# Five ring slots for the gathered rows, and the residual kept in its own memory

## The chip, the cores and the metric

One core of a Trainium2 chip runs the whole program, written in Bass with its waits and queues by hand. The metric is the device time of one execution in microseconds, median of the runs; the profile is one more execution.

## The reference, cut to what matters

One layer of a decoder over 512 prompt tokens and 64 sample tokens (8 sequences of 8), width 1024: a hybrid mixer, attention over memory tokens, then PEER, a layer of 16384 single-neuron experts. The change is in PEER:

```
q = (x @ wq).reshape(N, 8, 2, 64)                  # 8 heads, two half queries
s = einsum('thpd,hpkd->thpk', q, keys)             # 128 keys for each half
sv, si = top_k(s, 16); cv, ci = top_k(all 256 sums, 16)
eidx = i1 * 128 + i2                               # 8 x 16 = 128 experts a token
gate = softmax(cv)
h = gelu(sum_d u_tab[eidx] * x)                    # one dot product each
out = sum_k (gate * h) * v_tab[eidx];  y = rmsnorm(residual + out)
```

u_tab and v_tab have 16384 rows of 1024 floats, in float32.

## The kernel before, in words

hT holds the residual, transposed: 128 partitions x 8 blocks x 576 tokens. The mixer and the attention add to it. PEER then works on two groups of tokens in two ways.

**Dense.** The first 384 prompt tokens go through all experts. peer_experts runs 128 steps j: step j takes one 512 KB tile of the u table, in a high part (ACT, L1835) and a low part (POOL, L1803), multiplies it by the tokens in three products (PE, L1921), and ACT applies gelu (L1864) and stores the activations to DRAM (acts). peer_output runs 128 steps e over v (1 MB loads of two), weighted by activations times gates. DVE chooses the experts of these tokens (select) and spreads their gates into dense matrices from step FIRST_SPREAD = 85 on, three groups of four tokens to a step (L2078, L2080).

**Gathered.** The other 128 prompt tokens and the 64 sample tokens are done pick by pick: 128 picks for the prompt tokens, 64 for the samples (two halves of the picks on 128 partitions), 192 in all. For pick n (counted from 0) POOL fetches by an indirect DMA the 8 KB row (u and v side by side) of the expert of each of 128 partitions into a ring slot, 1 MB in all (fetch, L1514). DVE forms the dot product with u (product, L1521), ACT the gelu and the gate (weigh, L1527 and L1529), and DVE adds v times the weight to a sum (add, L1540); add of pick n-2 follows the product of pick n. A slot is free for fetch n when add of pick n - SLOTS is done; POOL waits for that.

SLOTS is 7. Five slots are memory of their own (40 KB a partition, which also serves peer_scores as nT and qT), and two lie in hT. Because these overwrite the residual, peer_scores stores hT whole to a DRAM tensor (saved, L1585), and SP waits for it. peer_output loads the columns it needs back into hC, in eight DMAs at the steps 1, 3, 5 and 7 (L2154, L2155), after a wait for the last stored activations, and PE adds them by products with the identity (L2236 after step 16, L2244 at the end).

**Order.** Every engine works its list in the order written. ACT's step j: wait until PE has finished the product of step j-1, gelu of it, the high part of tile j+2, a store, parts of the gates' spreading, then the weighings of the picks of step j. POOL's step j: the low part of tile j+2, then the fetches of step j. In the spread steps POOL first waits for DVE's one-hot matrices. pick_step(n) gives ACT's step for pick n: 20 + 4n/3 up to pick 45, step 84 for 46 and 47, one to a step for 48 to 79 (steps 85 to 116), two to a step for 80 to 99 (steps 117 to 126). POOL's step for fetch n is 13 for the first SLOTS of them, and else

```
before = n - gather.SLOTS
step = 13 if before < 0 else pick_step(min(before + 2, LOOP_PICKS - 1)) + 1
```

so with seven slots one step after the weighing of pick n-5. The picks 100 to 191 are worked in peer_output, three for every four steps, and there POOL has only fetches in its list. The picks and their order in time can be counted in the trace: the n-th instruction of L1514, L1521 or L1529 is that of pick n-1.

In peer_output DVE also makes the low part of every v row (L2264), the weighting (L2255) and its low part (L2259), ACT the high parts (L2192, L2198).

Of the kernel before, what the change touches and what calls it, by code (L numbers as in the profile page):

```python
# [24 lines left out]
P = 128  # L25
D = 1024
# [1454 lines left out]

class Gather:

    FIXED = 5
    SLOTS = 7

    def __init__(self, nc, ctx, sem, hT):
        sb = lambda n, s, dt=F32: ctx.enter_context(nc.sbuf_tensor("ga_" + n, s, dt))
        self.ring = sb("ring", [P, self.FIXED, 2 * D])
        h_flat = hT[:, :, :].rearrange("p k n -> p (k n)")  # L1490
        self.slots = [self.ring[:, i] for i in range(self.FIXED)] + \
                     [h_flat[:, i * 2 * D:(i + 1) * 2 * D] for i in range(self.SLOTS - self.FIXED)]
        self.flat = self.ring[:, :, :].rearrange("p a b -> p (a b)")
        self.x = sb("x", [P, 2, D])
        self.idx = sb("idx", [P, NPICK], U32)
        self.gate = sb("gate", [P, NPICK])
        self.dot = sb("dot", [P, NPICK])
        self.act = sb("act", [P, NPICK])
        self.weight = sb("weight", [P, NPICK])
        self.landed = [sem(f"ga_landed{i}") for i in range(self.SLOTS)]  # L1500
        self.dots, self.gelus, self.weights, self.summed = (sem("ga_dots"), sem("ga_gelus"), sem("ga_weights"),
                                                            sem("ga_summed"))
# [46 lines left out]
def peer_scores(nc, io, sem, hT, cst, gains, ps, xhi, xlo, scores, gather):  # L1549

    CHUNKS = 2 * DT + 3
    with ExitStack() as ctx:
        def sb(name, shape, dt=F32):
# [13 lines left out]
        score_mm, score_out, high, dve_seq = (sem("ps_score_mm"), sem("ps_score_out"), sem("ps_high"),  # L1567
                                              sem("ps_dve_seq"))
        doubled, q_zero, q_doubled = sem("ps_doubled"), sem("ps_q_zero"), sem("ps_q_doubled")
        turned, turned_out, acc_ready, saved = (sem("ps_turned"), sem("ps_turned_out"), sem("ps_acc_ready"),  # L1570
                                                sem("ps_saved"))
        ident = cst[:, C_ID:C_ID + P]
        block = ctx.enter_context(nc.Block())

        @block.sync
        def _(sp):
            w = io["peer_wq"].rearrange("(k p) c -> p k c", p=P)
            for m in range(KT):
                tiles.load(sp, m, w[:, :, m * P:(m + 1) * P])
                if m == 3:  # L1580

                    sp.wait_ge(keys_zero, 1)
                    sp.dma_start(kbd[0:64, :, 0:NKEY], io["keysT"][0:64]).then_inc(keys_loaded, 16)
                    sp.dma_start(kbd[64:P, :, NKEY:2 * NKEY], io["keysT"][64:P]).then_inc(keys_loaded, 16)
            sp.dma_start(io["saved"], hT[:, :, :]).then_inc(saved, 16)  # L1585
            sp.wait_ge(saved, 16)

        @block.gpsimd
        def _(pool):
# [497 lines left out]
                gather.add(dve, n, acc)  # L2087


def peer_output(nc, io, sem, cst, ps, scores, gather, first):  # L2090

    GROUPS = NKEY // 4
    HC = ND + NS
    with ExitStack() as ctx:
        def sb(name, shape, dt=F32):
            return ctx.enter_context(nc.sbuf_tensor("po_" + name, shape, dt))
# [4 lines left out]
        vhi = sb("vhi", [P, 4, D], F32R)  # L2101
        vlo = sb("vlo", [P, 4, D], F32R)
        w, g_sb = first.w, first.g
        whi = sb("whi", [P, 2, 4, ND], F32R)
        hC = sb("hC", [P, KT, HC])
        wlo = sb("wlo", [P, 2, 4, ND], F32R)
        acc_s = sb("acc_s", [P, D])
        gain = sb("gain", [P, D])
        y3 = sb("y3", [P, D])
        stat = sb("stat", [P, 3, 5])  # L2110
        v_loaded, hg_loaded, gg_loaded = first.v_loaded, first.w_loaded, first.g_loaded
        h_loaded, gain_loaded = sem("po_h_loaded"), sem("po_gain_loaded")
        v_high, v_low, weighted, w_high, w_low = (sem("po_v_high"), sem("po_v_low"), sem("po_weighted"),
                                                  sem("po_w_high"), sem("po_w_low"))
        products, whole = sem("po_products"), sem("po_whole")
# [17 lines left out]
        @block.sync  # L2133
        def _(sp):
            def load_v(m):
                if m >= 4:
                    sp.wait_ge(v_low, m - 2)
                sp.dma_start(v_pairs[m // 2 % 2][:, :, :], v_dram[:, m:m + 2, :]).then_inc(v_loaded[m // 2 % 2], 16)

            def load_w(q):  # L2140
                if q >= 2:
                    sp.wait_ge(w_low, q - 1)
                first.load_w(sp, io, q)
                first.load_g(sp, io, q)

            load_v(2)
            load_w(1)
            for e in range(NKEY):
                if e == 1:
                    for c in range(2):  # L2150
                        sp.wait_ge(first.h_stored[c], 16 * (NKEY // 4))
                if e in (1, 3, 5, 7):
                    k = e - 1
                    sp.dma_start(hC[:, k:k + 2, 0:ND], io["saved"][:, k:k + 2, 0:ND]).then_inc(h_loaded, 16)  # L2154
                    sp.dma_start(hC[:, k:k + 2, ND:HC], io["saved"][:, k:k + 2, SEQ:NT]).then_inc(h_loaded, 16)  # L2155
# [30 lines left out]
        @block.scalar  # L2186
        def _(act):
            def high(e):
                act.wait_ge(v_loaded[e // 2 % 2], 16 * (e // 4 + 1))
                if e >= 4:  # L2190
                    act.wait_ge(products, e - 3)
                act.copy(vhi[:, e % 4], v(e)).then_inc(v_high, 1)  # L2192

            def first_w(q):
                act.wait_ge(weighted, q + 1)
                if q >= 2:
                    act.wait_ge(products, 4 * q - 4)
                act.copy(whi[:, q % 2], w[:, q % 2]).then_inc(w_high, 1)  # L2198

            high(0)  # L2200
            first_w(0)
            high(1)
            high(2)
            for e in range(NKEY):
                if e + 3 < NKEY:
                    high(e + 3)
                if e % 4 == 1 and e // 4 + 1 < GROUPS:
                    first_w(e // 4 + 1)
                if e and pick_of[e - 1] is not None:
                    gather.weigh(act, pick_of[e - 1])  # L2210
                if e == DONE3 + 2:
                    root(act, 0)
            for i in range(1, 5):
                root(act, i)

        @block.tensor
        def _(pe):
            for e in range(NKEY):
                s = e // 4 % 2
                pe.wait_ge(v_low, e + 1)  # L2220
                pe.wait_ge(w_low, e // 4 + 1)
                for t in range(DT):
                    for n, (x, y) in enumerate(((whi, vhi), (whi, vlo), (wlo, vhi))):
                        for a in range(2):
                            mm = pe.matmul(ps[:, 2 * t + a, :], x[:, s, e % 4, t * P:(t + 1) * P],  # L2225
                                           y[:, e % 4, a * 512:(a + 1) * 512], start=(e == 0 and n == 0),
                                           stop=(e == NKEY - 1 and n == 2), skip_group_check=True)
                    if e == NKEY - 1:
                        mm.then_inc(whole, 1)
                if e < NKEY - 1:  # L2230
                    mm.then_inc(products, 1)
                if e == ADD_H:
                    pe.wait_ge(h_loaded, 16 * 8)
                    for t in range(DT):
                        for k in range(KT):
                            pe.matmul(ps[:, 2 * t + k // 4, (k % 4) * P:(k % 4 + 1) * P], hC[:, k, t * P:(t + 1) * P],  # L2236
                                      ident, start=False, stop=False, skip_group_check=True)
            pe.wait_ge(gather.summed, NPICK)
            pe.wait_ge(normed, 1)
            for a in range(2):  # L2240
                pe.matmul(ps[0:NS, 6 + a, :], cst[:, C_FOLD:C_FOLD + NS], acc_s[:, a * 512:(a + 1) * 512],  # L2241
                          start=True, stop=False, skip_group_check=True)
                for k in range(4):
                    mm = pe.matmul(ps[0:NS, 6 + a, k * P:(k + 1) * P], hC[:, 4 * a + k, ND:HC], ident,  # L2244
                                   start=False, stop=True, skip_group_check=True)
            mm.then_inc(whole, 1)

# [56 lines left out]
def build(nc, io):  # L2304
    with ExitStack() as ctx:
# [32 lines left out]
        memory_attention(nc, io, sem, hT, cst, gains, ps)  # L2338
        free_semaphores()
        with ExitStack() as peer:  # L2340
            gather = Gather(nc, peer, sem, hT)
# [7 lines left out]
            peer_output(nc, io, sem, cst, ps, scores, gather, first)  # L2349


def feature_major(a):
# [49 lines left out]
def make(nc, x):  # L2402
# [7 lines left out]
    io["saved"] = nc.dram_tensor("saved", [P, KT, NT], F32, kind="Internal").ap()  # L2410
    build(nc, io)
    return {"in_" + n: a for n, a in arrays.items()}

# [22 lines left out]
```

## Time and profile before

| | us |
|---|---|
| median of 3 runs | 2148.25 (2147.71 to 2152.55) |
| profiled execution | 2154.12 |
| its span, first to last instruction | 2152.2 |
| PE busy | 1941.1 |
| DVE busy | 1440.6 |
| ACT busy | 883.1 |
| POOL busy | 770.7 |
| DMA moved | 512.99 MB, mean 238 GB/s |

Busy times overlap, since the engines work side by side. PE's is modelled: a busy PE is not PE at its peak. What holds the kernel differs from stage to stage, so it is read by stretches of the span: the select stretch of peer_experts runs from the first fetch (966 us) to 1262, the spread stretch to 1497, its last steps to 1568, and peer_output from 1581 to the end. Times inside the trace count from the start of the span. The granted clock is the mean share of TensorE's full clock.

### The profile page before, as it was taken

How to read it: one execution, taken by the hardware profiler on the slowest of the kernel's cores; microseconds unless marked ns; L12 is line 12 of the kernel's file. 1: busy time of each engine (PE TensorE's matmuls, PEld its weight loads, DVE VectorE, ACT ScalarE, POOL GpSimd, SP SyncE). 2: the span in 40 equal slices, each digit the busy share in tenths (PEclk: the TensorE clock that was granted, in tenths of full speed). 3: DMA queues.
4: the chain of work that ended last, by engine and by line, in shares of the span. 5: the costliest groups of instructions: out<-in, count | busy, mean ns of one | idle time of the engine just before them, and what ended most of it. 6: DMA issues, size and time to landing. Idle time of an engine off the chain costs nothing. (4 is left out here: it accounts for less than half of the span.)

```text
span 2152.2 us, 29522 instructions
## 1 busy us (share of the span) xinstructions
PE 1941.1 (90%) x11347; PEld 1778.6 (83%) x11347; DVE 1440.6 (67%) x2524; ACT 883.1 (41%) x1749; POOL 770.7 (36%) x438
## 2 busy tenths in 40 slices
PE   4999689797899898899999999999659999999998
PEld 3999579686887697799999999999647888777776
DVE  3686554721413213397999979997658888888886
ACT  2355212123322123334344469998223344333343
POOL 0233032323430032166777755556512222222220
PEclk9899789788999999899999999999879999999999
DMA  4231101023643123158999979999989999999994
GB/s 128 65 79 53 47 1 31 1 93 109 214 138 136 60 58 104 60 166 316 366 362 366 364 268 375 376 373 373 402 337 394 401 396 398 400 400 379 390 401 153
DMA packets 211595, 512.99 MB, mean 238 GB/s; under 512 B 13312, under 2 KB 143104, under 8 KB 174592
## 3 DMA queue, kind: packets, MB, share of 16 engines
q1 hardware_dynamic: 172864, 259.43, 35.5%
q0 software_dynamic: 27648, 201.34, 23.3%
q10 hardware_dynamic: 10944, 50.34, 5.8%
q8 instruction: 91, 1.49, 0.3%
q14 instruction: 48, 0.39, 0.1%
HBM read 451.26 MB, written 59.80 MB: 237 GB/s over the span
## 5 line engine op out<-in xcount | busy, mean ns | idle before, releaser
L1803 POOL TENSOR_TENSOR ex_ulo<-ex_u,ex_uhi 128x1024 fp32r<-128x1024 f32 x128 | 307.1, 2401 | 262.8 <-ACT ex_uhi L1835 157.8
L1921 PE MATMUL ps<-xhi,ex_uhi 128*128 128x384 f32 x1024 | 356.6, 348 | 31.9 <-ACT ex_h L1864 20.1
L1921 PE MATMUL ps<-xlo,ex_uhi 128*128 128x384 f32 x1024 | 347.5, 339 | 0.0
L1921 PE MATMUL ps<-xhi,ex_ulo 128*128 128x384 f32 x1024 | 347.3, 339 | 0.0
L1514 POOL DMA_INDIRECT ga_ring<-in_uv,ga_idx x138 | 167.8, 1216 | 299.8 <-DVE po_acc_s L1540 168.4
L2225 PE MATMUL ps<-po_vhi,po_whi 128*128 128x512 f32 x768 | 240.2, 394 | 36.2 <-DVE po_wlo L2259 32.6
L2225 PE MATMUL ps<-po_vhi,po_wlo 128*128 128x512 f32 x768 | 238.7, 392 | 0.0
L2225 PE MATMUL ps<-po_vlo,po_whi 128*128 128x512 f32 x768 | 238.4, 392 | 0.0
L1921 PEld LDWEIGHTS ps<-xhi,ex_uhi 128*128 128x128 f32 x1024 | 196.7, 192 | 35.2 <-issue 22.5
L2225 PEld LDWEIGHTS ps<-po_vhi,po_whi 128*128 128x128 f32 x768 | 143.9, 189 | 73.1 <-issue 39.7
L1921 PEld LDWEIGHTS ps<-xlo,ex_uhi 128*128 128x128 f32 x1024 | 196.6, 192 | 0.0
L1921 PEld LDWEIGHTS ps<-xhi,ex_ulo 128*128 128x128 f32 x1024 | 196.1, 192 | 0.0
L2225 PEld LDWEIGHTS ps<-po_vhi,po_wlo 128*128 128x128 f32 x768 | 145.4, 189 | 30.7
L2225 PEld LDWEIGHTS ps<-po_vlo,po_whi 128*128 128x128 f32 x768 | 145.3, 189 | 30.7
L200 POOL TENSOR_TENSOR at_w_lo<-at_w_raw,at_w_hi 128x1024 fp32r<-128x1024 f32 x32 | 77.1, 2409 | 226.3 <-ACT at_w_hi L194 226.3
L2192 ACT CAST po_vhi<-po_v 128x1024 fp32r<-128x1024 f32 x64 | 66.8, 1044 | 194.3 <-DMA po_v<-in_peer_v 186.2
L1835 ACT CAST ex_uhi<-ex_u 128x1024 fp32r<-128x1024 f32 x128 | 133.2, 1041 | 21.9 <-DMA ex_u<-in_uT 21.9
L1864 ACT ACTIVATE ex_h<-ps 128x384 f32<-128x384 f32 x128 | 62.1, 485 | 168.3 <-PE ps L1921 168.3
L1540 DVE SCALAR_TENSOR_TENSOR ps<-ga_ring,ga_weight,ps 128x1024 f32<-128x1024 f32 x92 | 118.1, 1284 | 1.5 <-ACT ga_weight L1529 1.3
L2264 DVE TENSOR_TENSOR po_vlo<-po_v,po_vhi 128x1024 fp32r<-128x1024 f32 x64 | 78.1, 1221 | 58.7 <-ACT po_vhi L2192 58.6
L212 PE MATMUL ps<-at_nlo,at_w_hi 128*128 128x256 f32 (+1 forms) x512 | 106.1, 299 | 12.4 <-POOL at_w_lo L200 7.0
L200 POOL TENSOR_TENSOR in_w_lo<-in_w_raw,in_w_hi 128x1024 fp32r<-128x1024 f32 x24 | 59.0, 2460 | 156.1 <-ACT in_w_hi L194 156.1
(406 smaller groups left out, 4273.9 us busy)
## 6 DMA issues: line engine op xcount, KB each, us to landing
ex_u<-in_uT SPq DMA_DIRECT2D x128, 512.0 KB, 6.2
scores<-in_peer_v SPq DMA_DIRECT2D x32, 1024.0 KB, 9.9
po_v<-in_peer_v SPq DMA_DIRECT2D x32, 1024.0 KB, 11.8
acts<-ex_h ACTq DMA_DIRECT2D x64, 384.0 KB, 7.8
gates<-scores ACTq DMA_DIRECT2D x12, 2048.0 KB, 12.8
scores<-acts SPq DMA_DIRECT2D x32, 768.0 KB, 12.6
scores<-gates SPq DMA_DIRECT2D x32, 768.0 KB, 15.9
in_w_raw<-in_w_in SPq DMA_DIRECT2D x24, 512.0 KB, 4.1
```

What stands on the lines that cost most here:

```text
L200: pool.tensor_tensor(self.lo[m % 2], self.raw[:, m % 3], self.hi[m % 2].bitcast(F32), ALU.subtract).then_inc(self.low, 1)
L212: mm = pe.matmul(ps[:, 2 * slot + bank, 0:size], w[m % 2][:, k, :], x[:, k, c:c + size], start=(k == 0 and n == 0), stop=(k == KT - 1 and ...
L1514: pool.indirect_dma_start(self.slots[n % self.SLOTS], None, io["uv"][:, :], bass.IndirectOffsetOnAxis(ap=self.idx[:, n:n + 1], axis=0)).th ...
L1540: ins = dve.scalar_tensor_tensor(out=acc, in0=self.v(n), scalar=self.weight[:, n:n + 1], in1=acc, op0=ALU.mult, op1=ALU.add)
L1803: pool.tensor_tensor(ulo[:, j % 3], u[:, j % 3], uhi[:, j % 3].bitcast(F32), ALU.subtract).then_inc(low, 1)
L1835: act.copy(uhi[:, j % 3], u[:, j % 3]).then_inc(high, 1)
L1864: act.activation(h[:, c, (j - 1) % 2], ps[:, (j - 1) % 2, 0:ND], ACT.Gelu_apprx_tanh).then_inc(gelus, 1)
L1921: mm = pe.matmul(ps[:, j % 2, 0:ND], w[:, j % 3, k, :], x[:, k, :], start=(k == 0 and n == 0), stop=(k == KT - 1 and n == 2))
L2192: act.copy(vhi[:, e % 4], v(e)).then_inc(v_high, 1)
L2225: mm = pe.matmul(ps[:, 2 * t + a, :], x[:, s, e % 4, t * P:(t + 1) * P], y[:, e % 4, a * 512:(a + 1) * 512], start=(e == 0 and n == 0), st ...
L2264: dve.tensor_tensor(vlo[:, e % 4], v(e), vhi[:, e % 4].bitcast(F32), ALU.subtract).then_inc(v_low, 1)
```

## The change

The ring has five slots, all in its own memory. The residual stays in hT: its store to DRAM, SP's wait for that, the eight loads of it and the buffer hC go, and PE's additions read hT. The wait for the last stored activations goes from SP to ACT, ahead of the cast into whi of group 1, and the order of whi and wlo in memory is turned. Through SLOTS the place of each fetch from pick 5 on moves in POOL's order, to one step after the weighing of pick n-3.

```
--- before.py
+++ after.py
@@ -1481,15 +1481,12 @@
 
 class Gather:
 
-    FIXED = 5
-    SLOTS = 7
-
-    def __init__(self, nc, ctx, sem, hT):
+    SLOTS = 5
+
+    def __init__(self, nc, ctx, sem):
         sb = lambda n, s, dt=F32: ctx.enter_context(nc.sbuf_tensor("ga_" + n, s, dt))
-        self.ring = sb("ring", [P, self.FIXED, 2 * D])
-        h_flat = hT[:, :, :].rearrange("p k n -> p (k n)")
-        self.slots = [self.ring[:, i] for i in range(self.FIXED)] + \
-                     [h_flat[:, i * 2 * D:(i + 1) * 2 * D] for i in range(self.SLOTS - self.FIXED)]
+        self.ring = sb("ring", [P, self.SLOTS, 2 * D])
+        self.slots = [self.ring[:, i] for i in range(self.SLOTS)]
         self.flat = self.ring[:, :, :].rearrange("p a b -> p (a b)")
         self.x = sb("x", [P, 2, D])
         self.idx = sb("idx", [P, NPICK], U32)
@@ -1567,8 +1564,7 @@
         score_mm, score_out, high, dve_seq = (sem("ps_score_mm"), sem("ps_score_out"), sem("ps_high"),
                                               sem("ps_dve_seq"))
         doubled, q_zero, q_doubled = sem("ps_doubled"), sem("ps_q_zero"), sem("ps_q_doubled")
-        turned, turned_out, acc_ready, saved = (sem("ps_turned"), sem("ps_turned_out"), sem("ps_acc_ready"),
-                                                sem("ps_saved"))
+        turned, turned_out, acc_ready = sem("ps_turned"), sem("ps_turned_out"), sem("ps_acc_ready")
         ident = cst[:, C_ID:C_ID + P]
         block = ctx.enter_context(nc.Block())
 
@@ -1582,8 +1578,6 @@
                     sp.wait_ge(keys_zero, 1)
                     sp.dma_start(kbd[0:64, :, 0:NKEY], io["keysT"][0:64]).then_inc(keys_loaded, 16)
                     sp.dma_start(kbd[64:P, :, NKEY:2 * NKEY], io["keysT"][64:P]).then_inc(keys_loaded, 16)
-            sp.dma_start(io["saved"], hT[:, :, :]).then_inc(saved, 16)
-            sp.wait_ge(saved, 16)
 
         @block.gpsimd
         def _(pool):
@@ -2087,10 +2081,9 @@
                 gather.add(dve, n, acc)
 
 
-def peer_output(nc, io, sem, cst, ps, scores, gather, first):
+def peer_output(nc, io, sem, hT, cst, ps, scores, gather, first):
 
     GROUPS = NKEY // 4
-    HC = ND + NS
     with ExitStack() as ctx:
         def sb(name, shape, dt=F32):
             return ctx.enter_context(nc.sbuf_tensor("po_" + name, shape, dt))
@@ -2101,15 +2094,14 @@
         vhi = sb("vhi", [P, 4, D], F32R)
         vlo = sb("vlo", [P, 4, D], F32R)
         w, g_sb = first.w, first.g
+        wlo = sb("wlo", [P, 2, 4, ND], F32R)
         whi = sb("whi", [P, 2, 4, ND], F32R)
-        hC = sb("hC", [P, KT, HC])
-        wlo = sb("wlo", [P, 2, 4, ND], F32R)
         acc_s = sb("acc_s", [P, D])
         gain = sb("gain", [P, D])
         y3 = sb("y3", [P, D])
         stat = sb("stat", [P, 3, 5])
         v_loaded, hg_loaded, gg_loaded = first.v_loaded, first.w_loaded, first.g_loaded
-        h_loaded, gain_loaded = sem("po_h_loaded"), sem("po_gain_loaded")
+        gain_loaded = sem("po_gain_loaded")
         v_high, v_low, weighted, w_high, w_low = (sem("po_v_high"), sem("po_v_low"), sem("po_weighted"),
                                                   sem("po_w_high"), sem("po_w_low"))
         products, whole = sem("po_products"), sem("po_whole")
@@ -2146,13 +2138,6 @@
             load_v(2)
             load_w(1)
             for e in range(NKEY):
-                if e == 1:
-                    for c in range(2):
-                        sp.wait_ge(first.h_stored[c], 16 * (NKEY // 4))
-                if e in (1, 3, 5, 7):
-                    k = e - 1
-                    sp.dma_start(hC[:, k:k + 2, 0:ND], io["saved"][:, k:k + 2, 0:ND]).then_inc(h_loaded, 16)
-                    sp.dma_start(hC[:, k:k + 2, ND:HC], io["saved"][:, k:k + 2, SEQ:NT]).then_inc(h_loaded, 16)
                 if e == 19:
                     sp.dma_start(gain[:, :], io["final_g"].partition_broadcast(P)).then_inc(gain_loaded, 16)
                 if e % 2 == 0 and e + 4 < NKEY:
@@ -2195,6 +2180,10 @@
                 act.wait_ge(weighted, q + 1)
                 if q >= 2:
                     act.wait_ge(products, 4 * q - 4)
+                if q == 1:
+
+                    for c in range(2):
+                        act.wait_ge(first.h_stored[c], 16 * (NKEY // 4))
                 act.copy(whi[:, q % 2], w[:, q % 2]).then_inc(w_high, 1)
 
             high(0)
@@ -2230,10 +2219,9 @@
                 if e < NKEY - 1:
                     mm.then_inc(products, 1)
                 if e == ADD_H:
-                    pe.wait_ge(h_loaded, 16 * 8)
                     for t in range(DT):
                         for k in range(KT):
-                            pe.matmul(ps[:, 2 * t + k // 4, (k % 4) * P:(k % 4 + 1) * P], hC[:, k, t * P:(t + 1) * P],
+                            pe.matmul(ps[:, 2 * t + k // 4, (k % 4) * P:(k % 4 + 1) * P], hT[:, k, t * P:(t + 1) * P],
                                       ident, start=False, stop=False, skip_group_check=True)
             pe.wait_ge(gather.summed, NPICK)
             pe.wait_ge(normed, 1)
@@ -2241,7 +2229,7 @@
                 pe.matmul(ps[0:NS, 6 + a, :], cst[:, C_FOLD:C_FOLD + NS], acc_s[:, a * 512:(a + 1) * 512],
                           start=True, stop=False, skip_group_check=True)
                 for k in range(4):
-                    mm = pe.matmul(ps[0:NS, 6 + a, k * P:(k + 1) * P], hC[:, 4 * a + k, ND:HC], ident,
+                    mm = pe.matmul(ps[0:NS, 6 + a, k * P:(k + 1) * P], hT[:, 4 * a + k, SEQ:NT], ident,
                                    start=False, stop=True, skip_group_check=True)
             mm.then_inc(whole, 1)
 
@@ -2338,7 +2326,7 @@
         memory_attention(nc, io, sem, hT, cst, gains, ps)
         free_semaphores()
         with ExitStack() as peer:
-            gather = Gather(nc, peer, sem, hT)
+            gather = Gather(nc, peer, sem)
             scores = peer.enter_context(nc.sbuf_tensor("scores", [P, 16 * DT + 24, NKEY], F32))
             with ExitStack() as dense:
                 xhi = dense.enter_context(nc.sbuf_tensor("xhi", [P, KT, ND], F32R))
@@ -2346,7 +2334,7 @@
                 first = Firsts(sem, scores)
                 peer_scores(nc, io, sem, hT, cst, gains, ps, xhi, xlo, scores, gather)
                 peer_experts(nc, io, sem, cst, ps, xhi, xlo, scores, gather, first)
-            peer_output(nc, io, sem, cst, ps, scores, gather, first)
+            peer_output(nc, io, sem, hT, cst, ps, scores, gather, first)
 
 
 def feature_major(a):
@@ -2407,7 +2395,6 @@
 
     io["acts"] = nc.dram_tensor("acts", [NKEY // 4, P, 4, ND], F32, kind="Internal").ap()
     io["gates"] = nc.dram_tensor("gates", [ND // 32, P, P, 32], F32, kind="Internal").ap()
-    io["saved"] = nc.dram_tensor("saved", [P, KT, NT], F32, kind="Internal").ap()
     build(nc, io)
     return {"in_" + n: a for n, a in arrays.items()}
 
```

## Rows read from the trace of the kernel before

**Rows 1.** The page's first line.

```profile
span 2152.2 us, 29522 instructions
```

**Rows 2.** Windows: length; busy of PE, PEld, DVE, ACT, POOL; clock; DMA share, GB/s.

```profile
966.00:1262.00 296.00, 292.80 (x1685) 291.63 (x1684) 272.64 (x851) 125.82 (x238) 216.86 (x122) 1.00 0.93 352
...
1497.00:1568.00 71.00, 51.15 (x240) 49.08 (x238) 42.27 (x52) 20.54 (x55) 37.90 (x28) 0.83 1.01 401
...
1581.00:2152.00 571.00, 541.95 (x2372) 442.22 (x2372) 476.88 (x478) 222.99 (x362) 124.54 (x88) 0.98 0.98 372
```

**Rows 3.** Waits of 1497 to 1570: us, times, longest.

```profile
ACT ga_act L1527 <- DVE ga_dot L1521: 46.6, 16, 7.4
...
DVE ga_ring L1521 <- DMA ga_ring<-in_uv,ga_idx: 21.6, 11, 9.1
```

**Rows 4.** Timeline of one turn; last, from issue to landing of that fetch.

```profile
1521.34 0.48 ACT L1864 ACTIVATE ex_h<-ps 128x384 f32<-128x384 f32 x1
...
1522.83 2.41 POOL L1803 TENSOR_TENSOR ex_ulo<-ex_u,ex_uhi 128x1024 fp32r<-128x1024 f32 x1 [1.65 <-ACT ex_uhi L1835]
...
1525.38 0.95 POOL L1514 DMA_INDIRECT ga_ring<-in_uv,ga_idx  x1
...
1533.44 1.22 DVE L1521 CUSTOM_DVE_ANT_0 ga_ring<-ga_ring,ps 128x1024 f32<-128x1024 f32 x1 [1.90 <-DMA ga_ring<-in_uv,ga_idx]
...
1535.15 0.47 ACT L1864 ACTIVATE ex_h<-ps 128x384 f32<-128x384 f32 x1
...
DMA to landing us min/median/max: 8.0/8.0/8.0
```

**Rows 5.** Timeline, DVE: products of picks 83 and 99.

```profile
1497.44 1.22 DVE L1521 CUSTOM_DVE_ANT_0 hT<-hT,ps 128x1024 f32<-128x1024 f32 x1 [0.46 <-DMA hT<-in_uv,ga_idx]
...
1564.41 1.22 DVE L1521 CUSTOM_DVE_ANT_0 ga_ring<-ga_ring,ps 128x1024 f32<-128x1024 f32 x1 [0.94 <-DMA ga_ring<-in_uv,ga_idx]
```

**Rows 6.** Fetches of the select stretch, from issue to landing.

```profile
DMA to landing us min/median/max: 6.5/8.8/11.0
```

**Rows 7.** Products of picks 40 and 43, fetch 45 and its landing.

```profile
1213.65 1.21 DVE L1521 CUSTOM_DVE_ANT_0 hT<-hT,ps 128x1024 f32<-128x1024 f32 x1
...
1223.74 1.21 DVE L1521 CUSTOM_DVE_ANT_0 ga_ring<-ga_ring,ps 128x1024 f32<-128x1024 f32 x1
...
1224.16 0.95 POOL L1514 DMA_INDIRECT ga_ring<-in_uv,ga_idx  x1 [0.15 <-issue]
...
DMA to landing us min/median/max: 8.7/8.7/8.7
```

**Rows 8.** Waits of 1000 to 1250, and DVE's timeline at 1260.

```profile
ACT ga_act L1527 <- DVE ga_dot L1521: 35.7, 20, 6.4
...
1260.84 0.55 DVE L2061 TENSOR_REDUCE ex_total<-ex_drops 128x24 f32<-128x384 f32 x1 [9.09 <-ACT ex_drops L1877]
```

**Rows 9.** Product of pick 63, fetch 65 and its landing.

```profile
1375.52 1.21 DVE L1521 CUSTOM_DVE_ANT_0 ga_ring<-ga_ring,ps 128x1024 f32<-128x1024 f32 x1
...
1364.54 1.23 POOL L1514 DMA_INDIRECT ga_ring<-in_uv,ga_idx  x1
...
DMA to landing us min/median/max: 13.4/13.4/13.4
```

**Rows 10.** Product 161, fetch 163, its landing; DMA issues; SP's timeline.

```profile
1945.48 1.22 DVE L1521 CUSTOM_DVE_ANT_0 ga_ring<-ga_ring,ga_x 128x1024 f32<-128x1024 f32 x1
...
1930.92 1.68 POOL L1514 DMA_INDIRECT ga_ring<-in_uv,ga_idx  x1 [1.80 <-DVE po_acc_s L1540]
...
DMA to landing us min/median/max: 13.9/13.9/13.9
...
po_hC<-saved SPq DMA_DIRECT2D x4, 384.0 KB, 9.2
...
saved<-hT SPq DMA_DIRECT2D x1, 2304.0 KB, 10.7
...
1609.20 6.43 SPq L2154 DMA_DIRECT2D po_hC<-saved  x1
```

More of the change, by code:

```diff
@@ L1482, with __init__ @@
 class Gather:
-    FIXED = 5
-    SLOTS = 7
-    def __init__(self, nc, ctx, sem, hT):
+    SLOTS = 5
+    def __init__(self, nc, ctx, sem):
         sb = lambda n, s, dt=F32: ctx.enter_context(nc.sbuf_tensor("ga_" + n, s, dt))
[L1489 to L1492, printed above, removed]
+        self.ring = sb("ring", [P, self.SLOTS, 2 * D])
+        self.slots = [self.ring[:, i] for i in range(self.SLOTS)]
         self.flat = self.ring[:, :, :].rearrange("p a b -> p (a b)")
@@ L1569, in peer_scores @@
         doubled, q_zero, q_doubled = sem("ps_doubled"), sem("ps_q_zero"), sem("ps_q_doubled")
-        turned, turned_out, acc_ready, saved = (sem("ps_turned"), sem("ps_turned_out"), sem("ps_acc_ready"),
-                                                sem("ps_saved"))
+        turned, turned_out, acc_ready = sem("ps_turned"), sem("ps_turned_out"), sem("ps_acc_ready")
         ident = cst[:, C_ID:C_ID + P]
@@ L1584, in _ @@
                     sp.dma_start(kbd[64:P, :, NKEY:2 * NKEY], io["keysT"][64:P]).then_inc(keys_loaded, 16)
-            sp.dma_start(io["saved"], hT[:, :, :]).then_inc(saved, 16)
-            sp.wait_ge(saved, 16)
         @block.gpsimd
@@ L2087, in _, with peer_output @@
                 gather.add(dve, n, acc)
-def peer_output(nc, io, sem, cst, ps, scores, gather, first):
+def peer_output(nc, io, sem, hT, cst, ps, scores, gather, first):
     GROUPS = NKEY // 4
-    HC = ND + NS
     with ExitStack() as ctx:
@@ L2103, in peer_output @@
         w, g_sb = first.w, first.g
+        wlo = sb("wlo", [P, 2, 4, ND], F32R)
         whi = sb("whi", [P, 2, 4, ND], F32R)
-        hC = sb("hC", [P, KT, HC])
-        wlo = sb("wlo", [P, 2, 4, ND], F32R)
         acc_s = sb("acc_s", [P, D])
@@ L2111, in peer_output @@
         v_loaded, hg_loaded, gg_loaded = first.v_loaded, first.w_loaded, first.g_loaded
-        h_loaded, gain_loaded = sem("po_h_loaded"), sem("po_gain_loaded")
+        gain_loaded = sem("po_gain_loaded")
         v_high, v_low, weighted, w_high, w_low = (sem("po_v_high"), sem("po_v_low"), sem("po_weighted"),
@@ L2148, in _ @@
             for e in range(NKEY):
[L2149 to L2155, printed above, removed]
                 if e == 19:
@@ L2197, in first_w @@
                     act.wait_ge(products, 4 * q - 4)
+                if q == 1:
+                    for c in range(2):
+                        act.wait_ge(first.h_stored[c], 16 * (NKEY // 4))
                 act.copy(whi[:, q % 2], w[:, q % 2]).then_inc(w_high, 1)
@@ L2232, in _ @@
                 if e == ADD_H:
-                    pe.wait_ge(h_loaded, 16 * 8)
                     for t in range(DT):
                         for k in range(KT):
-                            pe.matmul(ps[:, 2 * t + k // 4, (k % 4) * P:(k % 4 + 1) * P], hC[:, k, t * P:(t + 1) * P],
+                            pe.matmul(ps[:, 2 * t + k // 4, (k % 4) * P:(k % 4 + 1) * P], hT[:, k, t * P:(t + 1) * P],
                                       ident, start=False, stop=False, skip_group_check=True)
@@ L2243, in _ @@
                 for k in range(4):
-                    mm = pe.matmul(ps[0:NS, 6 + a, k * P:(k + 1) * P], hC[:, 4 * a + k, ND:HC], ident,
+                    mm = pe.matmul(ps[0:NS, 6 + a, k * P:(k + 1) * P], hT[:, 4 * a + k, SEQ:NT], ident,
                                    start=False, stop=True, skip_group_check=True)
@@ L2340, in build @@
         with ExitStack() as peer:
-            gather = Gather(nc, peer, sem, hT)
+            gather = Gather(nc, peer, sem)
             scores = peer.enter_context(nc.sbuf_tensor("scores", [P, 16 * DT + 24, NKEY], F32))
@@ L2348, in build @@
                 peer_experts(nc, io, sem, cst, ps, xhi, xlo, scores, gather, first)
-            peer_output(nc, io, sem, cst, ps, scores, gather, first)
+            peer_output(nc, io, sem, hT, cst, ps, scores, gather, first)
 def feature_major(a):
@@ L2409, in make @@
     io["gates"] = nc.dram_tensor("gates", [ND // 32, P, P, 32], F32, kind="Internal").ap()
-    io["saved"] = nc.dram_tensor("saved", [P, KT, NT], F32, kind="Internal").ap()
     build(nc, io)
```

## The prediction

> **What bounds the kernel now.** I read the span first [rows 1]: 2152.2 us, against 2154.1 for the profiled execution, so 1.9 us lie around the span. Then the windows by stage [rows 2]. In the select stretch of peer_experts (966 to 1262 us) PE is busy 292.80 of 296.00 us, which makes PE and what feeds it the pace. In the last stretch of that function (1497 to 1568) PE is busy only 51.15 of 71.00 us and the clock is down to 0.83: something holds PE back. In peer_output (1581 to 2152) the DMA share is 0.98, so that function is bound by what its transfers move.
>
> What holds the last stretch is in its waits [rows 3]: ACT waits 46.6 us for DVE's dot products, and DVE waits 21.6 us for ring slots to land. Here the picks run at two to a step, and each is used the moment it lands. The timeline of one turn [rows 4] shows the order. ACT starts a step at 1521.34, makes the high part of a table tile, POOL the low part (1522.83), and only then, in its own order, does POOL issue the fetch (1525.38). It lands 8.0 us later; DVE multiplies at 1533.44, ACT weighs it, and only then ACT starts its next step, at 1535.15. This turn takes 13.81 us and **today carries two steps**: the fetch issued in step j is needed two steps on, because the seven slots let it go out five picks ahead of use. Nothing in the chain from ACT's step to the weighing can be left out, since ACT and POOL each take their work in the written order.
>
> **The rule for the fetches.** pick_step places fetch n one step after pick n-5 is weighed; with five slots that becomes pick n-3. So each new fetch n goes out where fetch n+2 goes out today, and lands where n+2 lands. The landing of n+2 minus the product of n is how late pick n will be. I applied this to every pick.
>
> **Late stretch, the main term.** Picks 80 to 99 are weighed in steps 117 to 126, two a step. With five slots the first fetch of step j is pick n, weighed in step j itself: step 118 weighs 82 and 83 and step 118 fetches 83 and 84. The turn of [rows 4] then carries **one** step. Start: pick 81 now waits for today's landing of 83, 1497.44 [rows 5], and with the 1.71 us from product to next step (1533.44 to 1535.15) ACT starts step 118 at 1499.15. Steps 118 to 125 are eight turns, 8 x 13.81 = 110.5; in step 126 pick 99 is multiplied 12.1 us after the start (1521.34 to 1533.44). Sum 1499.15 + 110.5 + 12.1 = 1621.8 for product 99, which today starts at 1564.41 [rows 5]: **+57 us**. The fetch's 8.0 us is the uncertain part. Shortest landing of the select stretch, with fewer bytes in flight, is 6.5 us [rows 6]: nine times 1.5 less, +44. The pair of it issued 1.26 us behind may keep it near that stretch's longest, 11.0: +84. I take 8.0, since two fetches, one table tile and a store in 13.8 us load the DMA less than today. PE does not take over: 240 matmuls are ten steps, 51.15 / 10 = 5.1 us each at clock 0.83, some 8.5 us at half speed, under 13.8.
>
> The Trainium skill, DMA: Bandwidth & Descriptors, section Anatomy of one DMA, gives a GpSimd-issued transfer about 2 us fixed plus its bytes over 436 GB/s, so an estimate by that page of 4.4 us for the 1 MB of a fetch. No fetch of the trace is that quick (6.5 at least, 8.0 in this turn), so the sum goes by the rows; by the page it would be 9 x 3.6 = 32 us less, 2208 in place of 2240.
>
> **Select stretch.** Today no product waits for a landing here. By the rule, 25 of the picks 5 to 45 are late, pick 43 the most: its product starts at 1223.74, and fetch 45 goes out at 1224.16 and lands 8.7 us later [rows 7], 9.1 us late. Were the schedule fixed, DVE would be at most 9.1 us late in all, and the 9.09 us for which DVE waits for ACT's exponentials at 1260.84 [rows 8] would hide it: lower end 0. But the schedule is not fixed: ACT already stands 35.7 us at 20 weighings [rows 8], so a late dot delays its step, that delays POOL's low part and the next fetch, and this feeds back. One such turn for three picks is 13.81 - 8.0 + 8.7 = 14.5 us, where DVE today goes from pick 40 to pick 43 in 10.1 us (1213.65 to 1223.74 [rows 7]). Seven stretches of three picks are that short (10.1 to 10.3), which gives 7 x 4.3 = 30 us as the upper end. PE forgives each late step about one step of its own, 4 us, as tiles are split two steps ahead. Adding lateness pick by pick from the rows, with every late weighing passed on after that allowance, I come close to the upper end. I take **+25**.
>
> **Spread stretch** (1262 to 1497), one pick in 6.84 us. Fetch n now goes out about 11 us before its product. Product 63 starts at 1375.52, fetch 65 today at 1364.54 landing 13.4 us later [rows 9]: 2.4 us late, the worst of the 31 picks. Twelve are late, by 15.7 us together; where two stand within two picks of each other the second profits from the first, which leaves 12. DVE and ACT take turns without a rest here, so I charge all of it: **+12**, from 4 (if ACT is ahead) to 18.
>
> **End of peer_experts.** Fetch 103 needs, with seven slots, the sum of pick 96, and goes out before product 99 starts. With five it needs the sum of pick 98, two sums after product 99 (their weighing takes the 1.71 us of [rows 4]), and the block's end waits for what is outstanding: **+2** (0 to 4).
>
> **peer_output.** Three picks go with four steps. The rule gives 85 picks that all land in time still, closest pick 161: product at 1945.48, fetch 163 today at 1930.92 landing 13.9 us later [rows 10], 0.7 us to spare; most have 2 to 4. Cost 0, up to 6 if landings lengthen. The removed loads of hC are 4 x 384 KB and 4 x 64 KB, 1.84 MB; at the 372 GB/s of this function [rows 2] that is 4.9 us, and as DMA is the bound it counts: **-5**. SP also stands 6.43 us in one of those issues [rows 10], ahead of a load of v, so down to -10. The wait for the stored h moves to ACT, ahead of whi of group 1. Queued behind it are ACT's further casts; DVE and PE wait for those. It asks for stores issued before the block began, and five casts of v go before it, so 0, up to 3. The store of h at the end of peer_scores (2304 KB, 10.7 us to landing [rows 10]) is issued when five of the eight weight tiles are split; the products of three tiles and all scores come behind it and hide it: 0. PE's additions of the residual read hT in place of hC, the same matmuls: 0.
>
> **Sum.** 25 + 12 + 57 + 2 - 5 = +91. On the profiled 2154.1 that is 2245; the median of the runs shown, 2148.25, is 5.9 lower, so 2240 to compare with it. Ends: 0 + 4 + 44 + 0 - 10 = +38, and 30 + 18 + 84 + 4 + 4 = +140; both at once are unlikely.
>
> **Rivals.**
> Short fetches: with three fetches in flight in place of five, landings shrink everywhere to the 6.5 us of [rows 6]. Late +44; a three-pick turn of 12.3 us makes the select bound 7 x 2.2 = 15, of which half, +8; spread +4, -5: +51, **2199**. For: the DMA moves 401 GB/s in the late stretch [rows 2], so queueing is in the 8.0. Against: the table tile and the stores still go beside it. Chance 0.22.
> Full feedback: landings of 11 us in the late stretch and the whole of the select bound: +30 + 18 + 84 + 4 = +136, **2284**. Against: bytes per us fall. Chance 0.09.
> Cover holds, faster: ACT's wait for a dot costs PE nothing because PE's two-step lead absorbs it, and only the 4.9 us of transfers remain: **2143**. This decides if the landing of n+2 comes before the product of n, or late weighings stay under the roughly 4 us lead; true in peer_output, false for all of the picks 80 to 99 (4.3 to 15.8 us late by the rule). Chance 0.03.
> No effect: the ring is no limit, since POOL's order alone paces the fetches, and saved bytes are lost elsewhere: 2148. Against: the step of each fetch is computed from SLOTS. Chance 0.02.
>
> **How the numbers follow.** The likeliest case has 0.64. 0.3% (6 us) is about what a measurement can tell here. Faster 0.03, same 0.02, slower 0.95. The range runs from the short-fetch case to just under full feedback, 2196 to 2278.
>
> **What would show it.** ACT's steps from 118 to 126 stand 13 to 15 us apart in place of 6 to 10, and DVE's wait for landings there grows from 21.6 us to some 80 us. Product 99 comes near 1660. Products of the select stretch, which wait for nothing today, wait for landings; step 85 comes some 25 us later. The fetch's landing in the late stretch stays near 8 us. peer_output takes about 566 us from its first load in place of 571, with no product that waits. I am wrong if the late steps keep their 8 us, or if select stays on time and the sum falls under +60.

## The result, and the profile after

The changed kernel takes 2218.06 us (median of 4 runs, 2217.71 to 2227.41) against 2148.47 us: ratio 1.0329, 95% interval 1.0307 to 1.0350, 69.6 us slower. Forecast: 2240, range 2196 to 2278.

First, the windows of the changed kernel over its own stretches (length; busy of PE, PEld, DVE, ACT, POOL; clock; DMA share, GB/s), to be laid beside [rows 2] (the first line is the page's):

```profile
span 2216.2 us, 29512 instructions
...
966.00:1285.00 319.00, 296.47 (x1667) 294.09 (x1666) 270.23 (x871) 121.67 (x234) 213.61 (x119) 0.97 0.86 315
1285.00:1525.00 240.00, 232.16 (x1601) 228.76 (x1600) 204.82 (x300) 221.56 (x618) 120.93 (x68) 1.00 0.91 345
1525.00:1640.00 115.00, 62.37 (x267) 59.72 (x265) 48.62 (x60) 23.33 (x62) 40.27 (x29) 0.78 0.73 273
1656.00:2216.00 560.00, 538.09 (x2372) 439.85 (x2372) 476.68 (x478) 221.91 (x362) 126.34 (x88) 0.99 0.98 376
```

In the last stretch of peer_experts the DMA share falls from 1.01 to 0.73 and the rate from 401 to 273 GB/s, while PE is busy 62.37 of 115.00 us. Neither is at its limit; the engines wait for one another. The waits of that stretch (us, times, longest; to [rows 3]):

```profile
ACT ga_act L1524 <- DVE ga_dot L1518: 90.0, 19, 10.9
DVE ga_ring L1518 <- DMA ga_ring<-in_uv,ga_idx: 67.8, 16, 9.0
POOL ex_ulo L1797 <- ACT ex_uhi L1829: 62.0, 9, 9.4
...
PE ps L1915 <- ACT ex_h L1858: 52.4, 8, 9.0
POOL ga_ring L1511 <- DVE ps L1537: 7.1, 2, 4.9
```

Read them as a closed circle of waits: ACT waits for the dot product, DVE for the landing, POOL for ACT's high part, PE for ACT's gelu. The wait for a free slot is the last line, 7.1 us in two fetches. The select stretch, where no product waited before, first from before (1000 to 1250) and then after (1000 to 1285):

```profile
PE ps L1921 <- ACT ex_h L1864: 0.6, 1, 0.6
```

```profile
ACT ga_act L1524 <- DVE ga_dot L1518: 98.5, 33, 11.7
...
DVE ga_ring L1518 <- DMA ga_ring<-in_uv,ga_idx: 33.4, 14, 4.4
...
PE ps L1915 <- ACT ex_h L1858: 21.6, 6, 7.8
```

So PE, which sets the pace there, now stands 21.6 us for ACT's gelu where it stood 0.6.

One turn of the late stretch, from ACT's, POOL's and DVE's timelines (start, us, engine), to [rows 4]; the last row is the landing of that fetch:

```profile
1585.46 0.47 ACT L1858 ACTIVATE ex_h<-ps 128x384 f32<-128x384 f32 x1
...
1586.94 2.37 POOL L1797 TENSOR_TENSOR ex_ulo<-ex_u,ex_uhi 128x1024 fp32r<-128x1024 f32 x1 [8.95 <-ACT ex_uhi L1829]
1589.46 0.95 POOL L1511 DMA_INDIRECT ga_ring<-in_uv,ga_idx  x1
...
1597.61 1.22 DVE L1518 CUSTOM_DVE_ANT_0 ga_ring<-ga_ring,ps 128x1024 f32<-128x1024 f32 x1 [8.95 <-DMA ga_ring<-in_uv,ga_idx]
...
1599.31 0.47 ACT L1858 ACTIVATE ex_h<-ps 128x384 f32<-128x384 f32 x1
...
DMA to landing us min/median/max: 8.1/8.1/8.1
```

It takes 13.85 us, as before (13.81), but the two gelus are those of **one** step apart, not two: between them ACT makes no other.

Where the 64.0 us between the two spans lie, read from the starts of ACT's gelus (L1864 before, L1858 after; the k-th is that of step k-1's product), the first cast of v and the span's end:

| stretch | before | after | change | predicted |
|---|---|---|---|---|
| up to the first gelu | 912.2 | 915.0 | +2.8 | 0 |
| select: first to 85th gelu | 354.1 | 380.2 | +26.1 | +25 |
| spread: 85th to 117th | 226.6 | 230.2 | +3.6 | +12 |
| late: 117th to 128th | 75.0 | 114.3 | +39.3 | +57 |
| to the first cast of v | 12.7 | 15.8 | +3.1 | +2 |
| peer_output | 571.8 | 560.7 | -11.1 | -5 |

The first line is noise: it varied from 905.5 to 915.1 among the runs below. The profiled execution of before was also 5.7 us over its median, which is why the medians lie 69.6 apart and the spans 64.0.

This table is one pair of profiles. Seven profiles below and here have this order of fetches in select and spread (the changed kernel, x1, x3, x7, x8, y1, y2): select takes 375.9 to 380.2, mean 378.0, and spread 230.2 to 233.9, mean 232.9. So select costs some 24 us and spread some 6, and the 3.6 of the table is the lowest of the seven. Late takes 112.9 to 116.9 in the five of them that keep it as it is (without x7 and x8), mean 114.8: 40 us.

### The profile page after: what moved, and what is told of

Read it like the earlier page. It is cut to its first block and busy times, and to the rows that moved or that the text cites. A ratio compares the mean times of both kernels' runs of the same rounds, so it can differ in the third digit from the quotient of the medians.

```text
span 2216.2 us, 29512 instructions
## 1 busy us (share of the span) xinstructions
PE 1953.2 (88%) x11347; PEld 1787.2 (81%) x11347; DVE 1437.3 (65%) x2524; ACT 880.3 (40%) x1749; POOL 771.3 (35%) x438
## 5 line engine op out<-in xcount | busy, mean ns | idle before, releaser
L1915 PE MATMUL ps<-xhi,ex_uhi 128*128 128x384 f32 x1024 | 362.3, 354 | 84.0 <-ACT ex_h L1858 74.0
L1511 POOL DMA_INDIRECT ga_ring<-in_uv,ga_idx x192 | 232.3, 1210 | 429.4 <-DVE po_acc_s L1537 246.0
L1518 DVE CUSTOM_DVE_ANT_0 ga_ring<-ga_ring,ps 128x1024 f32<-128x1024 f32 x100 | 121.6, 1217 | 111.6 <-DMA ga_ring<-in_uv,ga_idx 111.2
L1537 DVE SCALAR_TENSOR_TENSOR ps<-ga_ring,ga_weight,ps 128x1024 f32<-128x1024 f32 x128 | 164.4, 1285 | 0.2
L1524 ACT ACTIVATE ga_act<-ga_dot 128x1 f32<-128x1 f32 x192 | 38.2, 199 | 214.5 <-DVE ga_dot L1518 213.8
## 6 DMA issues: line engine op xcount, KB each, us to landing
scores<-gates SPq DMA_DIRECT2D x32, 768.0 KB, 15.8
```

What stands on the lines that cost most here:

```text
L1511: pool.indirect_dma_start(self.slots[n % self.SLOTS], None, io["uv"][:, :], bass.IndirectOffsetOnAxis(ap=self.idx[:, n:n + 1], axis=0)).th ...
L1518: dve.tensor_tensor_reduce(out=self.u(n), in0=self.u(n), in1=x, op0=ALU.mult, op1=ALU.add, scale=1.0, scalar=0.0, accum_out=self.dot[:, n: ...
L1524: act.activation(self.act[:, n:n + 1], self.dot[:, n:n + 1], ACT.Gelu_apprx_tanh).then_inc(self.gelus, 1)
L1537: ins = dve.scalar_tensor_tensor(out=acc, in0=self.v(n), scalar=self.weight[:, n:n + 1], in1=acc, op0=ALU.mult, op1=ALU.add)
L1915: mm = pe.matmul(ps[:, j % 2, 0:ND], w[:, j % 3, k, :], x[:, k, :], start=(k == 0 and n == 0), stop=(k == KT - 1 and n == 2))
```

## The experiments

Times are medians; ratios are to the kernel before on the same chip. Stretches are measured as in the table.

**x1: five slots, the residual stored and loaded as before.** Edit to the kernel before:

```
-    SLOTS = 7
+    SLOTS = 5
```

> The kernel before with SLOTS 5 alone: five own slots, the store of the residual and its eight loads stay. Theory (ring costs, transfers of the residual give back about 5 us): 2218 + 5 = 2223 us, with the same late steps of 11 to 14 us as the changed kernel. Rival A (the 11 us that peer_output was shorter in the changed kernel's profile all come from the missing loads): 2229. Rival B (the residual's transfers were hidden): 2218.

2223.96 us, ratio 1.0347 (1.0314 to 1.0379). Select 375.9, spread 232.7, late 112.9, peer_output 568.4. The ring alone costs all of the loss. What the residual's part gives back is taken up at y1 and y2.

**x2: six slots, residual stored.**

```
-    SLOTS = 7
+    SLOTS = 6
```

> The kernel before with SLOTS 6 (five own slots and one in hT). Theory (lateness of pick n is today's landing of fetch n+1 minus today's product of n): in the select stretch only 4 of 40 picks late, 5.4 us at most, which the schedule absorbs; spread none; late stretch: the second fetch of a pair now closes a turn of two steps, 1.3 us to 2.5 us longer a turn, four turns, 5 to 12 us. Total 2148 + 5 to 14 = 2153 to 2162. Rival (the cost is linear in the slots removed): half of the 75, near 2185.

2157.52 us, ratio 1.0044 (1.0020 to 1.0067): 8 us by the medians, 9 by the ratio, not half of 75. Select 353.9 and spread 226.6 are those of before; the late stretch takes 85.4 in place of 75.0. The rule by landings holds: one place of delay falls within the slack nearly everywhere, and two places do not.

**x3: seven slots, but the fetches in the order of five.**

```
-                step = 13 if before < 0 else pick_step(min(before + 2, LOOP_PICKS - 1)) + 1
+                step = 13 if before < 0 else pick_step(min(before + 4, LOOP_PICKS - 1)) + 1
```

> The kernel before, seven slots, but from fetch 7 on each fetch placed in POOL's order one step after the weighing of pick n-3 (pick_step(before + 4) in place of before + 2): memory of seven slots, order of five. Theory (the place in POOL's order makes the fetches late, not the slots' memory): as x1, 2215 to 2225, since picks 5 and 6 alone are fetched earlier. Rival (a free slot is what is missing): two free slots more remove the waits, 2148 to 2160.

2223.04 us, ratio 1.0334 (1.0317 to 1.0351), select 379.5, spread 233.0, late 114.8. Two free slots more change nothing. The waits of its late stretch, 1522 to 1638:

```profile
ACT ga_act L1527 <- DVE ga_dot L1521: 88.8, 19, 11.0
...
DVE ga_ring L1521 <- DMA ga_ring<-in_uv,ga_idx: 41.6, 9, 9.1
DVE hT L1521 <- DMA hT<-in_uv,ga_idx: 24.6, 5, 8.7
...
POOL ga_ring L1514 <- DVE ps L1540: 2.3, 1, 2.3
POOL hT L1514 <- DVE ps L1540: 1.5, 1, 1.5
```

41.6 + 24.6 = 66.2 us of waiting for landings against 67.8 in the changed kernel, and 3.8 us for slots. So the loss comes from the place of the fetches in POOL's list, which SLOTS happens to set, and not from the memory.

**x4: five slots, residual kept, and POOL's fetches ahead of its low part** from step 14 on, at the same step.

```
+                early = j > 13
+                if early:
+                    fetches(j)
                 if 0 < x < QUADS // PER_STEP:
                     pool.wait_ge(hots, PER_STEP * (x + 1))
...
-                for n in at.get(j, []):
-                    ...
-                    gather.fetch(pool, io, n)
+                if not early:
+                    fetches(j)
```

> The changed kernel, five slots, but from step 14 on POOL issues the fetches of a step ahead of the low part of that step. Theory (a turn is ACT's step start, high part, low part, fetch, landing, product, weighing; the first 4.0 us leave it): in the late stretch the fetch goes out as soon as the slot's sum is done, steps of about 8 us again, 25 to 35 us less; select lateness of at most 9 us falls by 3.5 us or more a pick, 20 us less; spread 3 less. 2218 - 50 = 2168, range 2155 to 2185. Rival (landings and slot reuse alone are the limit, POOL's order is not): within 10 us of 2218. Rival (POOL now stands in the slot's wait and its low parts come late, so PE starves): slower than 2218.

2156.8 us, ratio 1.0035 (1.0022 to 1.0048), 11 us better than expected: select 355.5, spread 225.5, late 79.5. The waits of its late stretch (1489 to 1569) have changed their kind:

```profile
ACT ga_act L1524 <- DVE ga_dot L1518: 54.6, 18, 10.0
POOL ga_ring L1511 <- DVE ps L1537: 36.2, 13, 8.7
DVE ga_ring L1518 <- DMA ga_ring<-in_uv,ga_idx: 35.3, 18, 8.1
```

Now POOL stands 36.2 us for free slots (7.1 in the changed kernel): with the fetches first, five slots do bind as memory. What they cost there is at most the distance to the kernels with fetches first and more slots, 79.5 against 66.9 (x5, six) and 65.3 (x6, seven). Those have their fetches one and two picks further ahead in POOL's list too, and no run here parts the two.

**x7: the same move, but only from step 118 on.** To x4:

```
-                early = j > 13
+                early = x > QUADS // PER_STEP
```

> The changed kernel, five slots; fetches ahead of the low part only from step 118 on. Theory (stages add up): select stays at 380 us from first to 85th step, spread at 230, late stretch 80 in place of 114, the rest as changed: 2218 - 34 = 2184, range 2178 to 2190. Rival (the lateness of the late stretch is handed down from the stretches before it): over 2195.

2186.01 us, ratio 1.0183 (1.0164 to 1.0201): select 379.2, spread 233.9, late 83.2. The stages add up to within a few us: select and spread stay as in the changed kernel, and the late stretch takes 83.2 here and 82.2 in y4, both behind a late spread stretch, against 79.5 in x4. It may inherit some 3 us; profiles of the same late stretch differ by up to 4.

**y4: x4, but in the spread steps the fetches stay behind the low part.** To x4:

```
-                early = j > 13
+                early = 13 < j < FIRST_SPREAD or x > QUADS // PER_STEP
```

> x4 (five slots, residual kept, fetches first) but in the spread steps 85 to 117 the fetches stand behind the low part as in the changed kernel. This leaves only the lateness of the spread stretch. Predicted term +12, all of it charged; measured in the changed kernel's profile +3.6 between ACT's steps 85 and 117. Theory now (DVE has 0.65 us of waiting on PE in each pick's time, by which it catches up): 4 to 7 us over x4's 2157, 2161 to 2164. Rival (every late product is charged): 2169.

2162.85 us, ratio 1.0081 (1.0044 to 1.0119). The median is 6 us over x4's, but the intervals touch; the spread stretch is clearer, with 231.9 us in place of 225.5. The waits between 1290 and 1490, of y4 first and of x4 (to 1480) second:

```profile
DVE scores L2079 <- PE ps L1902: 14.7, 24, 0.7
ACT ex_lookup L1841 <- DVE ex_lookup L2081: 8.3, 6, 2.9
DVE ga_ring L1518 <- DMA ga_ring<-in_uv,ga_idx: 8.1, 6, 2.9
```

```profile
DVE scores L2079 <- PE ps L1902: 17.3, 27, 0.7
```

DVE waits 8.1 us for landings and ACT then 8.3 us for DVE, and the stretch is 6 us longer. Three of DVE's short waits for PE are gone (17.3 to 14.7), so a small part is caught up. The rest of the gap to my 12 is that fewer products were late.

**x8: the table tiles from 118 on loaded to an eighth**, so their products are of old values.

```
+                    part = 1 if j + 2 >= 118 else KT
-                    sp.dma_start(u[:, (j + 2) % 3], io["uT"][j + 2])...
+                    sp.dma_start(u[:, (j + 2) % 3, 0:part], io["uT"][j + 2][:, 0:part])...
```

> The changed kernel, but the table tiles from 118 on are loaded to an eighth only (64 KB in place of 512), so their products use old values. Theory (the landing of a turn's fetch is 8.0 us beside a tile's load and 5.6 without one): the first fetches of the pairs in steps 119 to 122 land in 5.5 to 6 us, these turns fall from 13.8 to 11.4 us, 8 to 10 us less: 2208 to 2211. Rival (a landing is 8 us by itself while the pair's second fetch runs beside it): turns stay at 13.8, 2218.

2211.38 us (2 runs, ratio 1.0292, 1.0267 to 1.0318), against 2218 to 2219. Its median alone proves little, but the late stretch takes 108.0 us, under all five of the profiles without this edit (112.9 to 116.9). One turn, its timeline and the landing of its fetch:

```profile
1556.92 0.47 ACT L1859 ACTIVATE ex_h<-ps 128x384 f32<-128x384 f32 x1
...
1560.92 0.95 POOL L1511 DMA_INDIRECT ga_ring<-in_uv,ga_idx  x1
...
1566.56 1.22 DVE L1518 CUSTOM_DVE_ANT_0 ga_ring<-ga_ring,ps 128x1024 f32<-128x1024 f32 x1 [6.21 <-DMA ga_ring<-in_uv,ga_idx]
...
1568.26 0.47 ACT L1859 ACTIVATE ex_h<-ps 128x384 f32<-128x384 f32 x1
...
DMA to landing us min/median/max: 5.6/5.6/5.6
```

This turn takes 11.3 us, 5.6 of them the landing; the other 5.7 are the order. Two of the turns in question (those of picks 87 and 89) are so short. Pick 91's fetch landed in 7.6, and its turn stayed at 13.3. SP's timeline shows what went beside it: fetch 91 is issued at 1583.61, and behind it come the first loads of peer_output, which this edit left whole (the v load alone is 1 MB):

```profile
1584.00 0.33 SPq L1721 DMA_DIRECT2D scores<-acts  x1
1584.37 0.43 SPq L1724 DMA_DIRECT2D scores<-gates  x1
1584.84 6.31 SPq L1789 DMA_DIRECT2D scores<-in_peer_v  x1
```

These are the likely cause; no run without them was made.

**x6: the kernel before, seven slots, with the fetches first.** The edit is that of x4.

> The kernel before, seven slots and the residual stored, with the fetches of a step ahead of its low part. Theory (with seven slots nothing but the late stretch waits for landings, and there DMA share is 1.01 at 401 GB/s, so an earlier issue only lengthens the landings): within 6 us of 2148, the late stretch 75 us as now or up to 5 less. Rival (the turn of ACT, POOL and fetch still sets the late steps): late steps fall from 8.1 to 6.1 us, 2148 - 20 = 2128.

2143.35 us, ratio 0.9980 (0.9968 to 0.9991). The late stretch falls from 75.0 to 65.3, more than I allowed; the whole falls by 5.5. Windows of it, before and x6:

```profile
1492.80:1567.80 75.00, 55.35 (x264) 53.28 (x263) 44.93 (x56) 23.16 (x61) 40.43 (x29) 0.84 1.01 402
```

```profile
1492.30:1557.60 65.30, 50.55 (x264) 48.20 (x263) 43.57 (x55) 22.77 (x61) 39.53 (x28) 0.95 1.02 416
```

The rate rises by 3% only; 75.0 x 402 is 30.2 MB, 65.3 x 416 is 27.2 MB, so 3 MB left the stretch, and with it most of the time. A part was only put off: the first v load, issued by SP in this stretch, takes 40.4 us to land in place of 30.5. It now lands after the last fetch, and the way from the 128th gelu to the first cast of v grows from 12.7 to 15.1 us. Over both stretches that leaves 7.3 us. As I expected, the landings grow: fetches 80 to 99 take 13.8 us on average where they took 11.1. They start early enough for that not to matter. A full DMA was no proof that an earlier issue is worth nothing.

**x5: the version that the experiments point to.** Residual kept as in the changed kernel, six slots of their own memory, fetches first. Beside SLOTS = 6 and the edit of x4, memory for the sixth slot is made by sharing (the last line is in words):

```
-        kbd = sb("kbd", [P, PH, 2 * NKEY])
+        kbd = gather.flat[:, 2 * KT * NT:2 * KT * NT + PH * 2 * NKEY]...
-        drops = sb("drops", [P, DT * PICKS])
-        gpick = sb("gpick", [P, 2, PICKS])
-        pickT = sb("pickT", [P, 3, ND])
+        drops, gpick, pickT = columns of cst that PEER does not read
```

> Residual kept in hT as in the changed kernel, but six slots in memory of their own (keys in the ring's spare end during the scores; drops, gpick and pickT in constants that PEER does not read), and the fetches of a step ahead of its low part. Theory: no product of the select or spread stretch late beyond what the schedule absorbs, late steps of 7 to 8 us, and the residual's 4.2 MB of transfers gone: 2148 - 5 = 2143, range 2138 to 2150. Rival (six slots still cost their 8 us, as with the saved residual and the old order): 2152.

2140.21 us, ratio 0.9961 (0.9945 to 0.9977), 0.4% faster than the kernel before: select 352.3, late 66.9, peer_output 562.8. x6 has 2143.35 on the same chip, and the two intervals overlap.

**y1, y2, y3: the residual's transfers.** y1 is the changed kernel again and y2 is x1 again, both on one chip. y3, also on that chip, has x5's order and six slots with the residual stored; x5 ran on another chip. To x6:

```
-    SLOTS = 7
+    SLOTS = 6
```

> The changed kernel once more, on one chip with the next three. Theory (the residual's transfers are 4.9 us of peer_output): 5 us under y2 of the same chip. Rival (hidden): the same as y2 within 2 us.

> Five slots with the residual stored and loaded, on the same chip as y1. Theory: y1 + 5 us, the difference in peer_output. Rival: y1 within 2 us.

> x5 with the residual stored and loaded again: five own slots and one in hT, fetches ahead of the low part. Theory: the residual's 5 us more than x5's 2140, so 2145. Rival (the gain of x5 is the order's alone): 2140.

y1 2219.46 us, ratio 1.0320 (1.0294 to 1.0346); y2 2223.44, ratio 1.0336 (1.0310 to 1.0361); y3 2142.58, ratio 0.9965 (0.9949 to 0.9981). The medians give 4.0 us (y2 less y1) on one chip. For y3 less x5, on two chips, the ratios give 0.0004, under 1 us. Both have the sign expected, but each pair's intervals overlap, so the whole time does not show a gain. The profiles are clearer for the stretch itself. peer_output of y1 and y2, as windows:

```profile
1651.90:2212.50 560.60, 537.64 (x2372) 439.88 (x2372) 476.85 (x478) 222.47 (x362) 127.49 (x88) 0.99 0.98 375
```

```profile
1654.80:2223.50 568.70, 542.61 (x2372) 442.33 (x2372) 477.31 (x478) 222.59 (x362) 124.97 (x88) 0.98 0.98 373
```

Over all profiles, the seven with the loads have 571.8, 565.5, 568.4, 570.5, 566.9, 568.7 and 569.0 us, mean 568.7; the seven without 560.7, 565.8, 562.8, 564.5, 563.0, 560.6 and 560.1, mean 562.5: 6.2 us less. The two groups all but part (565.5 is the lowest of the one, 565.8 the highest of the other). How much of this reaches the whole time is open.

## Why the prediction was right, and where it was off

The whole: 2240 was forecast and 2218 measured, 22 us less. That is about as near to the rival "short fetches" (2199), so the time alone doesn't tell the two apart; the stretches do. Each term came with the sign and from the cause that was forecast, and two were too large: late by some 17 us, spread by 6 to 8.

**The rule for the fetches: right.** "Each new fetch n goes out where fetch n+2 goes out today" gave which stretches pay (select, late), which pay little (spread) and which not at all (peer_output: no product waits, the closest has 1.0 us to spare). x2 tests it for a delay of one place, and x3 shows that order and not memory is the cause.

**Late, +57 predicted, 39 measured: mechanism right, size off.** Two terms of the sum. (a) "8 x 13.81": the eight turns, from step 118 on, were 14.2, 11.6, 13.9, 13.7, 13.9, 11.2, 11.4 and 11.4, 101.3 in place of 110.5. In the turns of 13.7 to 13.9 us the fetch lands in 7.9 to 8.1, beside a tile's load. The last tile has been loaded by step 123, and from then on it lands in 5.5 to 5.6, under the 6.5 that I took as the least (x8 shows the same with the tiles made small). The second turn, of pick 85, doesn't fit: 5.9 us beside a whole tile's load, and I have no cause for it. (b) "in step 126 pick 99 is multiplied 12.1 us after the start": it came 4.2 us after. From step 126 on POOL has no low part left to make, so nothing holds its fetch back: 99, the third line below, goes out straight behind 97 and 98 of step 125,

```profile
1625.89 0.95 POOL L1511 DMA_INDIRECT ga_ring<-in_uv,ga_idx  x1 [0.15 <-issue]
1627.15 0.94 POOL L1511 DMA_INDIRECT ga_ring<-in_uv,ga_idx  x1 [0.30 <-issue]
1628.39 0.94 POOL L1511 DMA_INDIRECT ga_ring<-in_uv,ga_idx  x1 [0.30 <-issue]
...
1637.47 1.22 DVE L1518 CUSTOM_DVE_ANT_0 ga_ring<-ga_ring,ps 128x1024 f32<-128x1024 f32 x1 [0.39 <-DMA ga_ring<-in_uv,ga_idx]
```

These 7.9 us could be read in the loop's bound, and in the trace of before, where product 99 starts 4.0 us after the gelu of step 126. 9.2 + 7.9 is the 17 us missing.

The signs moved with it: DVE's waits for landings grew to 67.8 us and not to some 80, product 99 came at 1637.47 and not near 1660, and half of the late steps stood 11 to 12 us apart, not 13 to 15.

By the Trainium skill, DMA: Bandwidth & Descriptors, section Anatomy of one DMA, an estimate for such a fetch is 4.4 us. The quickest of all runs took 5.4, so turns worked out by the page would be too short by a us; for the last three turns (landings of 5.5 to 5.6) it was nearer than my 8.0.

**Select, +25 predicted, 26.1 measured (24 over seven profiles): right.** The feedback was the step in doubt (0 if the schedule were fixed). PE waits 21.6 us for ACT's gelu there now, and ACT 98.5 us for dots where it waited 35.7 [rows 8]. x4 removes it (355.5) by taking the low part out of the turn. That +25 was hit so closely is partly luck: it was a choice between 0 and 30.

**Spread, +12 predicted, 3.6 measured, 6 over seven profiles and by y4 and x4: too high.** The step was "I charge all of it". Twelve late products were foreseen and 7 or 8 waited, 8 to 10 us in all, and not all of that reached the time.

**End of peer_experts, +2: right** (3.1). **peer_output, -5: right** for the stretch, if a little more: 6.2 over the profiles. The -11 of the one pair is partly the profiled execution of before, whose stretch was the longest of the seven. The moved wait for the stores cost nothing that shows.

**The rival "short fetches"** (2199) was half true: landings did shrink, to 8.2 us on average over the late stretch from 11.1, but not in select (8.7 after and 8.7 before, fetches 7 to 47). "Cover holds" (2143), "no effect" (2148) and "full feedback" (2284) are excluded by the time.

## What to carry to other kernels

A constant that sizes a ring may also place the fetches in a queue's order. Before the change is priced as memory, ask which instruction stands ahead of the moved fetch on its engine: here it was one low part of 2.4 us and the cast before it, and putting the fetches ahead of them gave back 61 of 70 us with the five slots as they were (x4). To price a delay by k places, lay today's landing of n+k beside today's use of n, and then count turns: a fetch that misses its own step turns a chain shared by two steps into one for each. Read the loop's end too, where work that delays the fetch runs out.

## What the runs showed that I had not expected

A 1 MB gather of 128 rows of 8 KB lands 5.5 to 5.6 us after the start of its issue when only a second one goes beside it, 1.26 us behind (picks 93 and 95 of the changed kernel), and in 7.9 to 8.1 beside one 512 KB load as well (87, 89; 5.9 once, 85). It takes 11.1 on average when the DMA moves 402 GB/s, and 13.8 at 416 GB/s when the fetches go out earlier (x6). And a stretch whose DMA share reads 1.01 at 402 GB/s could still be shortened by 13% through order alone, of which a quarter came back in the next stretch (x6).
